# Grid and sparse attention: steps scored in unshifted pairs, both heads' turned short steps in one PSUM bank

## What is computed

```python
# sparse layer: a selected and a window branch, both causal here (512 tokens, window 512, top 8 of 8 blocks)
s_s = einsum('bqgjd,bgqkd->bgjqk', qblk, k_g) + bias_s
p_s = softmax(where(dist_s >= 0, s_s, NEG)); o_s = einsum('bgjqk,bgqkd->bqgjd', p_s, v_g)
s_w = einsum('bqgjd,bkgd->bgjqk', qblk, k_win) + bias_w
p_w = softmax(where(m_w, s_w, NEG));         o_w = einsum('bgjqk,bkgd->bqgjd', p_w, v_win)
o = gate[..., 0:1] * o_c + gate[..., 1:2] * o_s + gate[..., 2:3] * o_w
o = o * silu(z); y = o @ w_out

# grid layer: 8 rows x 64 columns, each query sees a window of 8 rows x 16 columns
s = einsum('bwhd,biwjhd->bhwij', q_r, k_win) * scale + bias
pr = softmax(s); o = einsum('bhwij,biwjhd->bwhd', pr, v_win)
y = (o * silu(z)) @ w_out
```

## Time and profile before

| | |
|---|---|
| median of 3 runs | 1495.37 us (1488.54 to 1497.93) |
| profiled execution | 1490.42 us, its span 1488.6 us |
| TensorE busy | 1391.8 us (93% of the span) |
| VectorE, ScalarE, GpSimd busy | 620.4, 712.6, 777.5 us (42, 48, 52%) |
| sparse attention | about 216 to 382 us of the span |
| grid attention | about 934 to 1010 us |
| latent attention | about 1260 to 1370 us |

### The profile page before, as it was taken

The page is one execution under the profiler, slowest core; times in us unless marked ns, Lnnn a source line. Parts: engine busy times, 40 slices in busy tenths (PEclk is TensorE's granted clock), DMA queues, the critical chain, the costliest instruction groups (busy, mean ns, idle before and its releaser), DMA issues.

```text
span 1488.6 us, 20916 instructions
## 1 busy us (share of the span) xinstructions
PE 1391.8 (93%) x7818; PEld 1133.3 (76%) x7818; DVE 620.4 (42%) x1602; ACT 712.6 (48%) x1522; POOL 777.5 (52%) x722
## 2 busy tenths in 40 slices
PE   6999999999989999888989999889999999999997
PEld 5877777777878888766778888768878787677785
DVE  3321067787151110596151110781442135888143
ACT  4242258887343223575342333882544244788252
POOL 5362356666445344365554433795646434566652
PEclk9999999999999999799999999899999999999999
DMA  6232310000433222111443232315224222001521
GB/s 235 85 114 85 114 57 30 30 30 1 156 110 145 101 97 87 55 44 43 170 138 117 90 109 85 142 58 212 99 85 184 85 85 85 2 1 41 201 85 57
DMA packets 27876, 139.57 MB, mean 94 GB/s; under 512 B 3328, under 2 KB 3712, under 8 KB 16128
## 3 DMA queue, kind: packets, MB, share of 16 engines
q1 hardware_dynamic: 14112, 98.57, 18.3%
q10 hardware_dynamic: 13664, 39.66, 7.7%
HBM read 129.83 MB, written 8.39 MB: 93 GB/s over the span
## 4 chain that ended last, share of the span: by engine, by line
PE 71%; POOL 10%; DVE 9%; ACT 5%; issue 2%; DMA 1%; ACTq 1%; POOLq 0%; SPq 0%; DVEq 0%
PE psum L379 57%; PE psum L1109 3%; POOL w_free L1249 3%; POOL w_lo L334 3%; PE psum L1092 3%; DVE w_free L1154 2%; PE psum L1068 2%; PE psum L827 2%; DVE u_lo L1167 2%; DMA w_raw<-in_weights 1%; POOL split L1266 1%; ACT w_hi L327 1%; PE psum L1081 1%; DVE arena L700 1%; ACT u_hi L1199 1%
## 5 line engine op out<-in xcount | busy, mean ns | idle before, releaser
L334 POOL TENSOR_TENSOR w_lo<-w_raw,w_hi 128x2048 fp32r<-128x2048 f32 (+1 forms) x111 | 425.5, 3846 | 462.4 <-ACT w_hi L327 462.0
L379 PE MATMUL psum<-u_lo,w_hi 128*128 128x512 f32 (+1 forms) x712 | 279.3, 392 | 4.2 <-DVE split L464 1.6
L379 PE MATMUL psum<-u_hi,w_lo 128*128 128x512 f32 (+1 forms) x712 | 277.6, 390 | 0.0
L379 PE MATMUL psum<-u_hi,w_hi 128*128 128x512 f32 (+1 forms) x712 | 277.6, 390 | 0.0
L327 ACT ACTIVATE w_hi<-w_raw 128x2048 fp32r<-128x2048 f32 x90 | 172.1, 1913 | 150.0 <-DMA w_raw<-in_weights 102.7
L379 PE MATMUL psum<-w_hi,split 128*128 128x512 f32 x608 | 196.0, 396 | 4.5 <-POOL w_lo L334 2.6
L748 ACT ACTIVATE w_free<-w_free,neg_max 128x256 f32<-128x256 f32 (+3 forms) x320 | 183.5, 580 | 6.3 <-DVE neg_max L1154 3.9
L379 PEld LDWEIGHTS psum<-u_lo,w_hi 128*128 128x128 f32 (+1 forms) x712 | 133.6, 188 | 33.7 <-issue 4.0
L379 PEld LDWEIGHTS psum<-u_hi,w_hi 128*128 128x128 f32 (+1 forms) x712 | 133.4, 187 | 28.8
L379 PEld LDWEIGHTS psum<-u_hi,w_lo 128*128 128x128 f32 (+1 forms) x712 | 133.5, 187 | 27.7
L379 PE MATMUL psum<-w_hi,u_lo 128*128 128x512 f32 (+2 forms) x352 | 135.6, 385 | 10.4 <-DVE u_lo L706 7.8
(11 more groups left out here) (188 smaller groups left out, 2190.0 us busy)
## 6 DMA issues: line engine op xcount, KB each, us to landing
w_raw<-in_weights SPq DMA_DIRECT2D x90, 1024.0 KB, 4.8
x<-x_scratch ACTq DMA_DIRECT2D x12, 512.0 KB, 6.5
gain<-in_gains ACTq DMA_DIRECT2D x10, 512.0 KB, 4.4
gain<-in_strips ACTq DMA_DIRECT2D x16, 256.0 KB, 3.0
spare<-in_strips ACTq DMA_DIRECT2D x16, 256.0 KB, 2.9
x_scratch<-x ACTq DMA_DIRECT2D x16, 256.0 KB, 4.1
gain<-in_near ACTq DMA_DIRECT2D x8, 512.0 KB, 4.3
w_raw<-in_near ACTq DMA_DIRECT2D x8, 512.0 KB, 3.8
```

The costliest lines, as they stand in the source:

```text
L334: low = nc.gpsimd.tensor_tensor(w_lo[b][:, c], w_raw[b][:, c], w_hi[b][:, c].bitcast(F32), ALU.subtract)
L379: mm = nc.tensor.matmul(dst, lhs, rhs, start=(a == 0 and k == 0 and (wl, ul) == (0, 1)), stop=(a + 1 == u and k + 1 == nk and (wl, ul) == ...
```

## The change

- TensorE's pairs of steps begin at an even step in the sparse and the grid layer (`shift` = 0): scores of steps 0 and 1, 2 and 3. The iteration is S(i), S(i+1), T(i-3), V(i/2 - 3), T(i-2), with i even, so the odd step is turned ahead of V and the even one behind it. The latent layer keeps `shift` = 1, the order of before.
- A step with at most 256 keys is "short". Both of its heads are turned into one bank, 4 + i % 2, the first head in columns 0 to 255, the second from 256 on. So successive short steps use different banks, and T(i) waits for low(i-2) where it waited for low(i-1). A long step keeps banks 4 and 5, one a head.
- For a short step one ScalarE and one VectorE instruction take out both heads, behind the turns of both.
- ScalarE's wait for V (semaphore `pv`) stands ahead of that for the turns.

```diff
-            def __init__(self, name, steps, branches):
+            def __init__(self, name, steps, branches, shift=0):
...
-        mla_flow = Flow("mla", full_steps(HEADS // 2), 1)
+        mla_flow = Flow("mla", full_steps(HEADS // 2), 1, shift=1)
...
+        def short(f, i):
+            return keys(f, i) <= 2 * P
+
+        def pt_bank(f, i, m):
+            return 4 + (i % 2 if short(f, i) else m)
+
+        def pt_place(f, i, m):
+            if short(f, i):
+                return psum[:, pt_bank(f, i, m), m * 2 * P:m * 2 * P + keys(f, i)]
+            return bank(pt_bank(f, i, m), keys(f, i))
+
+        def turned_both(f, i):
+            return bank(pt_bank(f, i, 0)).rearrange("p (m c) -> p m c", m=2)[:, :, 0:keys(f, i)]
+
+        def pt_both(buf, f, i):
+            c = pt_cols(i, 0, 1).start
+            return buf[:, c:c + 2 * T].rearrange("p (m c) -> p m c", m=2)[:, :, 0:keys(f, i)]
...
                 for m in range(2):
                     pe.wait_ge(f.p, 2 * i + m + 1)
-                    if i >= 1:
-                        pe.wait_ge(f.low, 2 * i + m - 1)
+                    before = [k for k in range(i) if pt_bank(f, i, m) in (pt_bank(f, k, 0), pt_bank(f, k, 1))]
+                    if before:
+                        k = before[-1]
+                        pe.wait_ge(f.low, 2 * k + 2 if short(f, k) else 2 * k + pt_bank(f, i, m) - 3)
...
-            for i in range(-1, f.steps + LAG + 1, 2):
+            for i in range(-f.shift, f.steps + 5 - f.shift, 2):
...
-                if i == f.steps + 1:
+                if i == f.steps + 2 - f.shift:
                     first_output(pe, f, 0)
                 if 0 <= i - LAG < f.steps:
                     turn(i - LAG)
-                d = (i - LAG) // 2 - 1
+                d = (i + f.shift) // 2 - LAG
                 if d >= 0:
                     values(d, 0)
                     values(d, 1)
                 if 0 <= i + 1 - LAG < f.steps:
                     turn(i + 1 - LAG)
...
             def low(i):
                 n = keys(f, i)
+                if short(f, i):
+                    dve.wait_ge(f.high, 2 * i + 2)
+                    nc.vector.tensor_tensor(pt_both(u_lo, f, i), turned_both(f, i), pt_both(u_hi, f, i).bitcast(F32), ALU.subtract)\
+                        .then_inc(f.low, 2)
+                    return
...
             def high(i):
                 n = keys(f, i)
+                if i >= 4:
+                    act.wait_ge(f.pv, 2 * (i // 2 - 1))
+                if short(f, i):
+                    act.wait_ge(f.turned, 2 * i + 2)
+                    nc.scalar.activation(pt_both(u_hi, f, i), turned_both(f, i), ACT.Copy).then_inc(f.high, 2)
+                    return
                 for m in range(2):
                     act.wait_ge(f.turned, 2 * i + m + 1)
-                    if i >= 4 and m == 0:
-                        act.wait_ge(f.pv, 2 * (i // 2 - 1))
```

More of the change, by code:

```diff
@@ L187, in _program @@
         class Flow:
-            def __init__(self, name, steps, branches):
+            def __init__(self, name, steps, branches, shift=0):
                 self.name, self.list, self.steps, self.branches = name, steps, len(steps), branches
-                self.groups = self.steps // (2 * branches)
+                self.groups, self.shift = self.steps // (2 * branches), shift
                 self.low_out, self.out_sum = sem(f"{name}_low_out"), sem(f"{name}_out_sum")
@@ L1088, in turn @@
                     pe.wait_ge(f.p, 2 * i + m + 1)
-                    if i >= 1:
-                        pe.wait_ge(f.low, 2 * i + m - 1)
+                    before = [k for k in range(i) if pt_bank(f, i, m) in (pt_bank(f, k, 0), pt_bank(f, k, 1))]
+                    if before:
+                        k = before[-1]
+                        pe.wait_ge(f.low, 2 * k + 2 if short(f, k) else 2 * k + pt_bank(f, i, m) - 3)
                     for kt in range(n // P):
-                        tr = nc.tensor.transpose(psum[:, 4 + m, kt * P:(kt + 1) * P], p_map(f, i, m, n)[:, kt * P:(kt + 1) * P], ident[:])
+                        tr = nc.tensor.transpose(pt_place(f, i, m)[:, kt * P:(kt + 1) * P], p_map(f, i, m, n)[:, kt * P:(kt + 1) * P], ident[:])
                     tr.then_inc(f.turned, 1)
@@ L1166, in low @@
                     c = pt_cols(i, m, n)
-                    nc.vector.tensor_tensor(u_lo[:, c], bank(4 + m, n), u_hi[:, c].bitcast(F32), ALU.subtract).then_inc(f.low, 1)
+                    nc.vector.tensor_tensor(u_lo[:, c], pt_place(f, i, m), u_hi[:, c].bitcast(F32), ALU.subtract).then_inc(f.low, 1)
             def add_out(g):
@@ L1194, in high @@
                 n = keys(f, i)
+                if i >= 4:
[4 more added lines that the diff above has]
+                    return
                 for m in range(2):
                     act.wait_ge(f.turned, 2 * i + m + 1)
-                    if i >= 4 and m == 0:
-                        act.wait_ge(f.pv, 2 * (i // 2 - 1))
-                    nc.scalar.activation(u_hi[:, pt_cols(i, m, n)], bank(4 + m, n), ACT.Copy).then_inc(f.high, 1)
+                    nc.scalar.activation(u_hi[:, pt_cols(i, m, n)], pt_place(f, i, m), ACT.Copy).then_inc(f.high, 1)
             def low_out(g):
```

## The result

Twenty runs of each kernel in turn gave a median of 1500.03 us (1494.21 to 1508.75) where the kernel before had 1490.62 (1486.03 to 1498.57, and one run of 5176.62 that stands alone and does not move the median); the ratio is 1.0055, with a 95% interval of 1.0036 to 1.0075. That is about 8 us more (5 to 11), within the one per cent called "the same" and inside the range of 1485 to 1507, 4 us above the forecast. The profiled execution took 1497.98 us (span 1496.2) against 1490.42, so 7.6 us more, where the sum had 1.5. That 1496 came within 4 us of 1500 is in part luck: the change itself was forecast at 1.5 us and came at 8, and the median of three that the forecast was added to (1495.37) lay 4.8 us over the median of twenty.

What follows compares the result with a forecast made beforehand. TensorE with stalls before turns was taken to bound sparse attention, GpSimd and an equally long second loop grid attention. -3.0 + 4.5 us, 1.5 on the median, gave 1497, written as 1496 us; range 1485 to 1507.

Steps and rivals of the forecast that it cites:

- the same: Whole kernel: a time within one per cent, 15 us, of before; given a chance of 0.90.
- the sum: Whole kernel: sparse attention 3.0 us faster plus grid attention 4.5 us slower, 1490.4 to 1491.9 us.
- second loop: Grid attention: loop through TensorE, ScalarE and VectorE, as long as GpSimd's, would grow from 4.27 to 4.82 us.
- 0.15 us more latency per step: Merged short steps: "high" starts 0.12 us later, runs 0.06 shorter, and the addition is 0.09 later.
- the prediction's equation: Grid attention: x = 4.82 - (4.365 + x), so each half stretch lengthens by 0.23 us, 3.2 us over some 14.
- The waits of T(5) and T(6): Sparse unit: stalls left in front of these turns, 0.3 us (plus 0.3 between heads) and 0.15 us.
- The new wait of S(3): Sparse unit: these scores wait for VectorE's score reading, queued behind low(5); 0.35 us.
- the fill: Start of sparse attention, first score to first output copy: no term in the forecast, so 16.55 us as before.
- I take 0.4 us back: End of sparse attention: T(61) waits longer without two scores before it, reducing the 3.4 us gain to 3.0.
- taken as a rule: Both stages: the skill's advice on breaking up instructions, by itself, says both lose from the merge; no size given.
- Gain: Rival: sparse stalls before turns go almost whole, grid stays at 8.73 us; -8 to -10 us, 1486; chance 0.17.
- Slower: the odd scores: Rival: sparse S(3), S(7), S(1) wait behind "low" in VectorE's queue; 12 to 17 us more, 1509; chance 0.13.

Runs made afterwards that it cites:

- e1: The change's new order in both stages, but each head in its own bank with separate instructions; 1496.99 us, 1.0049 against before.
- e9: The change with grid attention in the old order and only its even steps merged; 1495.46 us in one run, four grid steps 9.14 us.
- e5: The change reduced to the new order in sparse attention, no merge anywhere, grid attention as before; 1490.37 us, 1.0003 against before.
- e11: As e3, common bank, but two "highs" and two "lows" per short step behind both heads' turns; 1490.24 us in one run.
- e3: The change with grid attention alone put back to the old order, merge kept; 1492.39 us, 1.0021 against before.
- e4: The change with four additional, overwritten score products per step in grid attention; 1492.83 us, 1.0031 against before.
- e6: e5 with sparse attention's first output product one iteration (two steps) earlier; 1482.98 us, 0.9962 against before.
- e7: The change without ScalarE's wait on V in front of "high"; 1494.72 us, 1.0041 against before.
- e2: The change's banks and merged instructions in the order of before; 1492.38 us, 1.0024 against before.
- e8: The change with eight additional score products in each of sparse attention's first eight steps; 1502.76 us, 1.0097 against before.

## Why the prediction was right, and where it was not

**Right by mechanism in grid attention.** The second loop is the bound, it goes through V, T(even), "high", addition and reciprocal as written, and GpSimd idles in front of the even normalising. The forecast was 8.9 to 9.3 us for four steps; it is 9.39. The mis-sized term is the merge, "0.15 us more latency per step": it is 0.38. From T(odd) to the even normalising the loop is 0.69 us longer (5.37 against 4.68) where 0.55 was forecast. By the starts in the timeline, T(even) stands 2.05 us behind T(odd) where it stood 1.74 behind; that is the order, 0.31 us for the 0.40 given. "High" starts 0.74 us after T(even) instead of 0.48; the forecast was 0.60, the length of the four turns alone, without the 0.12 us that pass from their end to its start. The addition starts 1.42 us after "high" instead of 1.30, where 1.33 was forecast. These two are the merge, and the runs split the loop in the same way: 0.34 for the order alone (e1, 5.02), 0.35 more with the merge. At the odd step "high" is late too, 1.01 us after the start of T instead of 0.48, but it isn't on the path: the exponentials behind it end 2.50 us after T(odd), the even "high" starts at 2.79, and e9 without it costs the same. That a lateness counts half in each half stretch held: with 0.69 in place of 0.55 the prediction's equation gives 0.30 us, and 0.33 came.

**Right in a unit of sparse attention.** 19.4 us was forecast and 19.34 measured. The waits of T(5) and T(6), 0.3 and 0.15 us in the forecast, are 0.27 and 0.15; T(0) no longer waits; the waits on "low" went under 2 us. The new wait of S(3) behind "low", priced at 0.35 us, does not show in a unit.

**Wrong at both ends of the stages.** The stage is the fill, 6.5 units (the sum had 7.5) and the last two intervals. The units give 6.5 x 0.58 = 3.8 us less. One step that failed is "At the stage's end T(61) no longer has two scores before it and waits longer; I take 0.4 us back": the last two intervals are 1.45 us longer than before, where a unit is 0.58 shorter, so 2.0 go back. T(61), before and after:

```profile
368.72 1.40 PE L1092 MATMUL psum<-ident,w_free 128*128 128x128 f32 x8 [0.99 <-POOL w_free L1249]
```

```profile
367.81 1.40 PE L1112 MATMUL psum<-ident,w_free 128*128 128x128 f32 x8 [1.13 <-POOL w_free L1278]
```

Its wait is only 0.14 us longer. The larger part is a V of 1.1 us: before it stood ahead of that wait (366.61), now it stands behind T(61) (368.97 to 370.08), in what TensorE has left. The working priced this displaced V at the end of grid attention, 1.3 us, and left it out here. The other step is the fill, which the sum put at nothing without a reason, and which is 4.3 us longer. Together 1.9 us more; the stage has 1.7 more, where 3.0 less was forecast. e5 shows that the order alone can shorten the stage, by 1.8 us (by nothing in e1, whose fill met the low clock); the shared bank gave this back in the fill. The Trainium skill (Perfetto Trace Analysis, section Optimizing Scalar/DVE Operations) says that where ScalarE or VectorE isn't saturated but makes bubbles on other engines, breaking instructions up may let work finish sooner; taken as a rule it had said that both stages lose from the merge. The runs agree in the sign: 0.41 us per four steps in grid attention, 0.09 per unit and the fill in sparse attention. But e11 shows that it is the shared bank's wait, and not the longer instruction: two instructions behind both turns took 9.19 us, one 9.14.

**Missing: the clock.** The sum had no term for it. The risk could be read in the earlier trace rows: grid attention had 0.94 over its 80 us already, with TensorE idle 1.3 of 8.7 us, and a longer loop makes it idler. It cost some 6.4 us in this stage, more than the 5.8 of loop and end, for which the sum had 3.2 + 1.3. And it worked the other way in a stage that no edit touches: between the sparse and the grid stage the kernel after took 543.3 us and the one before 548.8. The window of 605 to 640 us has clock 0.85 after (row above); before it had

```profile
605.00:640.00 35.00, 30.65 (x174) 24.39 (x173) 24.99 (x97) 22.31 (x80) 15.51 (x28) 0.66 0.10 32
```

By these clocks the low stretch lasted some 24 us there and 10 after. Over the eleven experiments the time between the two stages is 543.3 to 544.1 in e3, e4, e6 and e7, 547.9 to 549.1 in e1, e2, e5, e8 and e9, and 545.9 and 554.1 in the other two; no property of the edits sorts them so. So the profiled 7.6 us are +1.7 (sparse), +11.2 (grid) and -5.5 (between), with 0.2 in what is left, and single executions, of which a stage without an edit moved by up to 11 us, can't be compared closer than some 5 to 10 us. The medians of e5 (1490.37) and e1 (1496.99), 6.6 us apart (0.46% by their ratios to before, on two chips), are safer ground: the two kernels differ in the order of grid attention alone, and their traces differ there by 6.4 us (83.82 - 77.46).

**The rivals.** "Gain" fell for the kernel as a whole; but the argument against it, that the 5.9 us of waits on GpSimd stay, was too strict: they are 2.9 us after, and 4.6 with the order alone (e5). "Slower: the odd scores" was right in its mechanism at one place only, the fill, where a score waits 1.88 us for VectorE; in the units the cover was long enough. The kernel is slower by 0.55%, which is under the one per cent that the chances went by, yet outside what 20 runs leave in doubt.

## What to carry to other kernels

Price a merge from the end of its last producer to the start of its consumer, not by the length of the instructions: putting two producers in one bank makes each consumer wait for the later of the two, and the saved instruction (0.07 us here) is small beside it (0.4 us per four steps). Price the fill and the drain of a reordered pipeline by themselves; here they decided the sign in a stage whose repeating part gained as forecast. Where a piece of work moves from ahead of the last wait to behind it, as V did, look for it at the end of every reordered stage. Where an edit makes TensorE idler in a stage that already shows a granted clock under 1.0, give the clock a term of its own, and try products without use there before undoing the edit.

## What was not expected of the hardware

- The spread between runs of one and the same program goes with the clock. Over the 20 runs after, time and mean granted clock have a correlation of -0.94: 1494.4 us at 0.981, 1508.75 at 0.966, so 0.01 of mean clock goes with about 10 us.
- 128 products without use shortened grid attention by 6.4 us (clock 0.83 to 0.98), and the kernel's loss against before from 0.55 to 0.31% (1500.03 and 1492.83 us). In sparse attention's fill the same trick raised the clock to 1.00 and gained nothing (20.65 against 20.82 us), since there a wait on VectorE decides; the whole kernel was at 1502.76 in four runs.
- The stages between the two attentions took from 543.3 to 554.1 us, in kernels that have the same instructions there.
